# Mixture of experts on one core: the 48-row block of the down product in plain fp32 on two column halves, and a second buffer for the raw down weights

## The chip, the cores and the metric

The kernel runs on one core of a Trainium2 chip. The metric is the device time of one execution in microseconds. Engines: TensorE (PE; its weight loads are PEld), VectorE (DVE), ScalarE (ACT), GpSimd (POOL), and SyncE (SP), whose queue issues most DMAs. Most executions of one kernel agree within 0.3%.

## What is computed

One decoder layer over 1024 positions of width 1024: a mixer of three head groups, cross-attention to 256 memory tokens, and a grouped mixture of experts, each followed by a layer norm. The change touches the last part alone:

```
scores = sigmoid(t @ router_w)               # 16 experts in 4 groups
group  = best group by the sum of its two best biased scores
expert_idx = the two best experts of that group; gate = their scores / their sum
for e in range(16):
    h = silu(t @ w_gate[e]) * (t @ w_up[e])  # 1024 -> 256
    y = y + combine[:, e:e + 1] * (h @ w_down[e])   # 256 -> 1024
x = layer_norm(alpha * x + y)
```

All arrays are fp32.

## The kernel before

The kernel has six phases (`project`, `prepare`, `attend`, `cross_attend`, `experts`, `overflow`), each a block in which every engine runs its own program and waits on semaphores. `cross_attend` ends by scattering each token's row of x (1024 values and its gates) to two slots of a DRAM table, `slot_rows`: one of the 176 slots (`CAP`) of each of its two experts. `experts` then goes over the 16 experts in turn, 176 rows each, as a block of 128 rows and a block of 48 (`ROWS`, `B1`). The 16 turns are written as a `step` per engine; `steps` runs the first four and the last two outright and the other ten in a hardware loop of two steps per turn. The order of the work is the order of each engine's program; there is no planner.

The experts run in the order first of each of the four groups, second of each, and so on, and a token's two experts lie in one group. A step adds the weighted down product to the rows that came with the expert and stores the sum (z) in `slot_sums`. In the first four steps (`NG`, `lowest`) that is all. From the fifth on, POOL first gathers, for each row whose token had its other expert earlier, that expert's stored sum (`gather_low`, L1873), and after the sum the step takes the layer norm, and POOL scatters it to the output for the rows that are now complete (L1900).

TensorE in one step, in order (`step` from L1940):
- gate and up product (L1948) in plain fp32: 32 products of 128 weight columns and 176 moving columns, into the banks `hps`;
- `turn` (L1929, L1931): transposes of the next expert's rows, of which 8 are 128 x 128 and 8 are 48 x 48, after a wait for `rows_loaded`;
- `down` (L1953 to L1962): the product of h (256) with the down weights (two halves of 512 output columns). h and the weights are split into a high part rounded to fp32r and a low part, and hi·hi + hi·lo + lo·hi is summed: 3 products for each of 2 halves of the contraction (`f`), and of the four `UNITS`: (128 rows, columns 0 to 511), (128 rows, 512 to 1023) and the same of the 48 rows. That is 24 products in fp32r of 512 moving columns each. The units use the PSUM banks 0, 1, 2 and 0 of `yps`, so the fourth waits until VectorE has taken the first (`z_made`).

A plain fp32 product appears in the trace as two records each of LDWEIGHTS and MATMUL, an fp32r product as one.

ScalarE takes silu, rounds h (L2002), copies the transposed rows to `xgT`, rounds the next expert's down weights (L1988, `split_down`) and takes squares for the norm (L2015). VectorE multiplies silu by up (L2072), takes the low part of h (L2074), makes the layer norm's output of the expert before (L2041), adds and weighs the four units as they leave PSUM (L2091, `z_made`), centres them (L2052) and takes the low part of the next down weights (L2026).

SP's queue in one step, in order: the raw down weights of the next expert (1 MB) into the only buffer `dn_raw`, after the split of this expert's (L1835); gate and up weights (2 MB) of the expert after next, after this gate and up product (L1838); two stores of z (L1842); the two fetches of the rows of the expert after next (`fetch`, L1824), 128 rows and 48 rows. As the wait for the split of the next weights comes late in the step, the down load of a step follows the row fetches of the step before.

In the retention of `prepare`, TensorE also has products of 64 rows of contraction (L527), whose operands lie in partitions 0 to 63 for two heads and 64 to 127 for the other two; in program order both of the first come ahead of both of the second.

Of the kernel before, what the change touches and what calls it, by code (L numbers as in the profile page):

```python
# [6 lines left out]
f32 = mybir.dt.float32  # L7
# [8 lines left out]
P = 128  # L16
# [15 lines left out]
CAP = 176  # L32
# [1143 lines left out]
def cross_attend(nc, k):  # L1176
# [73 lines left out]
    with nc.psum_tensor("x_tps", [P, 2, 512], f32) as tps, nc.psum_tensor("x_qps", [P, 512], f32) as qps, \  # L1250
# [6 lines left out]
        @block.sync  # L1257
        def _(sp):
            sp.wait_ge(q_lo, KD)
            for s in range(XH):  # L1260
                sp.dma_start(rawo[:, s, :], A["xa_wo"][s * P:(s + 1) * P, :]).then_inc(o_loaded, 16)
            sp.dma_start(rw[:], A["router_w"].rearrange("(s p) e -> p s e", p=P)).then_inc(rw_loaded, 16)
            sp.dma_start(rb[:], over(A["router_bias"], [P, NE])).then_inc(loaded, 16)
            sp.wait_ge(v_sum, 2)
            sp.dma_start(g[:], over(A["ln_xa_g"], [P, D])).then_inc(loaded, 16)
            sp.dma_start(b[:], over(A["ln_xa_b"], [P, D])).then_inc(loaded, 16)

            sp.wait_ge(w_lo, XH)
            sp.dma_start(k.e_dn[:], A["w_dn"][0].rearrange("s p n -> p s n")).then_inc(k.dn_loaded, 16)
# [472 lines left out]
def experts(nc, k):  # L1742
# [10 lines left out]
    g, b_ = k.g3, k.b3  # L1753
    gate_up, dn_raw = k.e_gu, k.e_dn
    xT = k.xgT
    hh = at("h", 143, [P, 2, CAP])
    act_g = at("silu_g", 144.5, [P, 2, CAP])
    hhi = at("h_hi", 146, [P, 2, CAP], f32r)
    hlo = at("h_lo", 147.5, [P, 2, CAP], f32r)
    slot_id = at("slot_number", 149, [P, NE, 2])  # L1760
# [25 lines left out]
    UNITS = [(0, 0), (0, 1), (1, 0), (1, 1)]  # L1786
    BANK = [0, 1, 2, 0]

# [21 lines left out]
    with nc.psum_tensor("rowsT_ps", [P, 3, 512], f32) as tps, nc.psum_tensor("h_ps", [P, 2, 512], f32) as hps, \  # L1810
# [3 lines left out]
        @block.sync  # L1814
        def _(sp):
            k.any_over["sp"] = sp.value_load(k.over_flag[0:1, 0:1], min_val=0, max_val=2 * S)
            def hold(sem, value):

                sp.wait_ge(sem, value)
                sp.sem_inc(held_sp, 1)  # L1820

            def fetch(row, b):
                for c in range(2):
                    sp.dma_start(rows[b][0:ROWS[c], c, :], k.xs_dram[bass.ds(row + c * P, ROWS[c]), :]).then_inc(rows_loaded[b], 16)  # L1824

            sp.wait_ge(k.rows_scattered, 16 * 2 * NT)
            sp.wait_ge(fields_cleared, 2)
            for e in range(2):
                fetch(e * CAP, e)

            def step(n, h, g_, e, b):
                last = is_one_of_last(e, 1)
                if not last:
                    hold(dn_lo_done, n(4, 4))
                    sp.dma_start(dn_raw[:], A["w_dn"][bass.ds(n(1, 1), 1)].rearrange("a s p n -> p (a s) n")).then_inc(dn_loaded, 16)  # L1835
                if not is_one_of_last(e, 2):
                    hold(gsum, n(2, 2))
                    sp.dma_start(gate_up[:, b], A["w_gu"][bass.ds(n(1, 2), 1)].rearrange("a s p n -> p (a s) n")).then_inc(gu_loaded[b], 16)  # L1838
                hold(z_stored, n(32, 128))
                for c in range(2):  # L1840
                    hold(z_made, n(4, 2 * c + 6))
                    sp.dma_start(k.z_dram[bass.ds(n(CAP, c * P), ROWS[c]), :], z[c][:]).then_inc(z_stored, 16)  # L1842
                if not is_one_of_last(e, 2):
                    hold(placed_at, n(1, 1))
                    fetch(n(CAP, 2 * CAP), b)

            steps(sp, step)
# [77 lines left out]
        def _(pe):  # L1925
# [12 lines left out]
            def step(n, h, g_, e, b):  # L1938
# [15 lines left out]

                def down(u, f):
                    c, j = UNITS[u]
                    w = 2 * f + j
                    hi, lo = (t[:, f, c * P:c * P + ROWS[c]] for t in (hhi, hlo))
                    out = yps[0:ROWS[c], BANK[u], :]
                    pe.matmul(out, hi, dn_hi[:, b, w, :], start=(f == 0), stop=False)  # L1960
                    pe.matmul(out, hi, dn_lo[:, b, w, :], start=False, stop=False)  # L1961
                    return pe.matmul(out, lo, dn_hi[:, b, w, :], start=False, stop=(f == 1))  # L1962

                pe.wait_ge(dn_lo_done, n(4, 4))
                pe.wait_ge(hlo_done, n(2, 1))
                for u, free in ((0, 4), (1, 2), (2, 3)):
                    pe.wait_ge(z_made, n(4, free))
                    down(u, 0)
                pe.wait_ge(hlo_done, n(2, 2))
                for u in range(3):  # L1970
                    down(u, 1).then_inc(ysum, 1)
                pe.wait_ge(z_made, n(4, 5))
                down(3, 0)
                down(3, 1).then_inc(ysum, 1)

# [3 lines left out]
        def _(act):  # L1979
# [6 lines left out]
            def split_down(b):  # L1986
                for s in range(4):
                    act.activation(dn_hi[:, b, s, :], dn_raw[:, s, :], ACT.Copy).then_inc(dn_hi_done, 1)  # L1988

            act.sem_inc(ysum, 8)  # L1990
            act.wait_ge(stats_cleared, 6)
            act.wait_ge(dn_loaded, 16)
            split_down(0)
            def step(n, h, g_, e, b):
                last = is_one_of_last(e, 1)
                for m in range(2):
# [4 lines left out]
                    act.wait_ge(ysum, n(4, 8))  # L2001
                    act.activation(hhi[:, m, :], hh[:, m, :], ACT.Copy).then_inc(hhi_done, 1)  # L2002
# [18 lines left out]
        def _(dve):  # L2021
            k.any_over["dve"] = dve.value_load(k.over_flag[0:1, 0:1], min_val=0, max_val=2 * S)
            def split_down(b, n):
                for s in range(4):
                    dve.wait_ge(dn_hi_done, n(4, s + 1))
                    dve.tensor_tensor(dn_lo[:, b, s, :], dn_raw[:, s, :], dn_hi[:, b, s, :].bitcast(f32), ALU.subtract).then_inc(dn_lo_done, 1)  # L2026

# [40 lines left out]
            def step(n, h, g_, e, b):  # L2068
                last = is_one_of_last(e, 1)
                for m in range(2):  # L2070
                    dve.wait_ge(silu, n(2, m + 1))
                    dve.tensor_tensor(hh[:, m, :], act_g[:, m, :], hps[:, m, CAP:2 * CAP], ALU.mult).then_inc(hmul, 1)  # L2072
                    dve.wait_ge(hhi_done, n(2, m + 1))
                    dve.tensor_tensor(hlo[:, m, :], hh[:, m, :], hhi[:, m, :].bitcast(f32), ALU.subtract).then_inc(hlo_done, 1)  # L2074
                    if last:
# [199 lines left out]
def program(nc, A, upto=99):  # L2275
# [47 lines left out]
    k.e_dn = at("e_down_raw", 89, [P, 4, 512])  # L2323
    k.gu_loaded, k.dn_loaded = [k.sem("gate_up_loaded_even"), k.sem("gate_up_loaded_odd")], k.sem("down_loaded")
    k.g3, k.b3 = at("ln3_g", 97, [P, D]), at("ln3_b", 101, [P, D])
# [57 lines left out]
```

## Time and profile before

| | |
|---|---|
| median of 3 runs | 1002.26 us (999.42 to 1003.21) |
| profiled execution, span | 1000.8 us |
| TensorE busy | 967.3 us, 97% |
| weight loads busy | 833.9 us, 83% |
| VectorE busy | 590.3 us, 59% |
| ScalarE busy | 350.6 us, 35% |
| GpSimd busy | 190.4 us, 19% |
| mean granted TensorE clock | 0.992 |
| gate and up product of the experts (L1948) | 155.4 us busy |
| DMA | 151.60 MB, mean 151 GB/s |

The profile is one execution; its own time is its span, from the first to the last instruction. Busy times of one engine overlap those of the others and are shares of that span. The experts' phase runs from about 720 us to the end. In the trace, a matmul record's length includes the way through the array, so records of back-to-back matmuls overlap; the distance from start to start is what one costs. A load's time "to landing" counts from its issue.

### The profile page before, as it was taken

Reading aid. Unit: us, or ns where it says so; the run is one execution under the profiler, and the core shown is the slowest. Engines: PE = TensorE matmul, PEld = TensorE weight load, DVE = VectorE, ACT = ScalarE, POOL = GpSimd, SP = SyncE. Lnnn points to the kernel's source line nnn. Section 1 sums busy time; section 2 is a strip of 40 time slices with the busy share of each in tenths; the row PEclk is TensorE's granted clock in tenths of the full one; section 3 lists DMA queues with packets and bytes.
Section 4 is the critical chain, followed back from the end, with each engine's and each line's share of the span. In section 5 each row is a group of like instructions: output and inputs, shape, how many; then the busy total and the mean of one; then the engine's idle time right before and its main releaser. Section 6 shows DMA issues by size and latency. Waiting matters only on the chain. (4 is left out here: it accounts for less than half of the span.)

```text
span 1000.8 us, 15741 instructions
## 1 busy us (share of the span) xinstructions
PE 967.3 (97%) x5687; PEld 833.9 (83%) x5687; DVE 590.3 (59%) x1271; ACT 350.6 (35%) x737; POOL 190.4 (19%) x248
## 2 busy tenths in 40 slices
PE   7999999999899999999999999999999999999995
PEld 6899888777778999988886888888888989898984
DVE  7744341678466666555557455458634376767676
ACT  6123031435365444430005333331223243434342
POOL 0012100112042110002220000002400134343335
PEclk9999999999899999999999999999999999999998
DMA  9122010001799200160023200032788888989872
GB/s 310 52 85 84 1 64 1 1 1 55 290 412 355 97 22 23 64 253 1 1 84 109 105 1 1 1 129 101 294 276 297 269 311 284 305 306 323 320 277 94
DMA packets 67278, 151.60 MB, mean 151 GB/s; under 512 B 8720, under 2 KB 16144, under 8 KB 67216
## 3 DMA queue, kind: packets, MB, share of 16 engines
q1 hardware_dynamic: 59920, 133.82, 38.0%
q0 software_dynamic: 7296, 16.95, 4.4%
q8 instruction: 39, 0.64, 0.3%
q14 instruction: 23, 0.19, 0.1%
HBM read 107.62 MB, written 52.03 MB: 160 GB/s over the span
## 5 line engine op out<-in xcount | busy, mean ns | idle before, releaser
L1948 PEld LDWEIGHTS h_ps<-xgT,e_gate_up 128*128 128x128 f32 x1024 | 153.9, 190 | 4.5 <-issue 2.2
L1948 PE MATMUL h_ps<-xgT,e_gate_up 128*128 128x176 f32 x1024 | 155.4, 313 | 2.2 <-DVEq L2056 2.2
L262 PE MATMUL unit_ps<-whi,xhi 128*128 128x512 f32 (+1 forms) x256 | 98.3, 384 | 6.2 <-DVE wlo L294 6.2
L263 PE MATMUL unit_ps<-wlo,xhi 128*128 128x512 f32 (+1 forms) x256 | 98.0, 383 | 0.0
L264 PE MATMUL unit_ps<-whi,xlo 128*128 128x512 f32 (+1 forms) x256 | 98.0, 383 | 0.0
L1001 PEld LDWEIGHTS o_ps<-mla_v,prob_T 128*128 128x128 f32 x576 | 70.0, 193 | 9.3 <-issue 6.0
L1001 PE MATMUL o_ps<-mla_v,prob_T 128*128 128x64 f32 x576 | 71.5, 274 | 3.7 <-ACT prob_T L1073 3.5
L262 PEld LDWEIGHTS unit_ps<-whi,xhi 128*128 128x128 f32 x256 | 48.7, 190 | 13.8 <-DVE xlo L338 6.1
L2091 DVE SCALAR_TENSOR_TENSOR z<-y_ps,slot_weight,x_rows 128x512 f32<-128x512 f32 (+1 forms) x64 | 45.7, 746 | 21.7 <-PE y_ps L1962 20.8
L264 PEld LDWEIGHTS unit_ps<-whi,xlo 128*128 128x128 f32 x256 | 48.6, 190 | 7.9
L263 PEld LDWEIGHTS unit_ps<-wlo,xhi 128*128 128x128 f32 x256 | 48.7, 190 | 7.7
L1960 PE MATMUL y_ps<-e_dn_hi,h_hi 128*128 128x512 f32 (+1 forms) x128 | 52.0, 406 | 0.1
L1962 PE MATMUL y_ps<-e_dn_hi,h_lo 128*128 128x512 f32 (+1 forms) x128 | 50.2, 392 | 0.0
L1061 ACT ACTIVATE prob<-s_ps,neg_max 128x640 f32<-128x640 f32 (+3 forms) x32 | 30.5, 954 | 56.2 <-issue 52.6
L1961 PE MATMUL y_ps<-e_dn_lo,h_hi 128*128 128x512 f32 (+1 forms) x128 | 50.1, 391 | 0.0
L1138 DVE COPY prob_T<-t_ps 128x512 f32<-128x512 f32 (+3 forms) x48 | 30.0, 624 | 21.9 <-PE t_ps L988 21.8
L2072 DVE TENSOR_TENSOR h<-silu_g,h_ps 128x176 f32<-128x176 f32 x32 | 10.6, 333 | 53.0 <-ACT silu_g L1999 53.0
L2015 ACT ACTIVATE ln_junk<-z,z_neg_mean 128x1024 f32<-128x1024 f32 (+1 forms) x24 | 27.6, 1150 | 40.8 <-DVE z_neg_mean L2046 37.5
L1999 ACT ACTIVATE silu_g<-h_ps 128x176 f32<-128x176 f32 x32 | 10.2, 318 | 89.3 <-PE h_ps L1948 82.0
L1122 DVE TENSOR_TENSOR s_ps<-s_ps,constants 128x128 f32<-128x128 f32 (+1 forms) x48 | 16.5, 343 | 40.4 <-PE s_ps L979 25.4
L2026 DVE TENSOR_TENSOR e_dn_lo<-e_down_raw,e_dn_hi 128x512 fp32r<-128x512 f32 x64 | 39.8, 678 | 0.8 <-ACT e_dn_hi L1988 0.8
L988 PE MATMUL t_ps<-constants,prob 128*128 128x128 f32 x288 | 40.1, 276 | 0.0
(337 smaller groups left out, 2133.1 us busy)
## 6 DMA issues: line engine op xcount, KB each, us to landing
e_gate_up<-w_gu SPq DMA_DIRECT2D x16, 2048.0 KB, 10.4
e_down_raw<-w_dn SPq DMA_DIRECT2D x16, 1024.0 KB, 5.6
slot_rows<-zeros SPq DMA_DIRECT2D x22, 522.0 KB, 6.2
slot_sums<-zeros SPq DMA_DIRECT2D x22, 512.0 KB, 6.3
x_rows<-slot_rows SPq DMA_DIRECT2D x16, 522.0 KB, 4.7
slot_sums<-z SPq DMA_DIRECT2D x16, 512.0 KB, 4.4
wraw<-w_in SPq DMA_DIRECT2D x24, 256.0 KB, 4.8
xraw<-xT SPq DMA_DIRECT2D x16, 256.0 KB, 4.9
```

Source lines behind the costliest of these rows:

```text
L262: pe.matmul(o, hi, whi[:, s, 0:w], start=(s == 0), stop=False)
L263: pe.matmul(o, hi, wlo[:, s, 0:w], start=False, stop=False)
L264: last = pe.matmul(o, lo, whi[:, s, 0:w], start=False, stop=(s == KD - 1))
L988: last = pe.transpose(tps[:, j, m * P:(m + 1) * P], prob[:, u % 2, j, m * P:(m + 1) * P], ident)
L1001: last = pe.matmul(ops[:, i % 2, h * MV:(h + 1) * MV], probT[:, u % 2, j, (m - a) * P:(m - a + 1) * P], k.v[:, m, h * MV:(h + 1) * MV], st ...
L1061: act.activation(prob[:, u % 2].rearrange("p j n -> p (j n)")[:, 0:(i + 1) * P], sps[:, u % 2].rearrange("p j n -> p (j n)")[:, 0:(i + 1) ...
L1948: end = pe.matmul(hps[:, m, gu * CAP:(gu + 1) * CAP], gate_up[:, b, s, w], xT[:, s, :], start=(s == 0), stop=(s == KD - 1))
L1960: pe.matmul(out, hi, dn_hi[:, b, w, :], start=(f == 0), stop=False)
L1961: pe.matmul(out, hi, dn_lo[:, b, w, :], start=False, stop=False)
L1962: return pe.matmul(out, lo, dn_hi[:, b, w, :], start=False, stop=(f == 1))
L2026: dve.tensor_tensor(dn_lo[:, b, s, :], dn_raw[:, s, :], dn_hi[:, b, s, :].bitcast(f32), ALU.subtract).then_inc(dn_lo_done, 1)
L2091: dve.scalar_tensor_tensor(z[c][:, f], yps[r, BANK[u], :], wgt[r, b, c:c + 1], rows[b][r, c, f], ALU.mult, ALU.add, accum_out=zsum[r, c, j ...
```

## The change

The 48-row block no longer uses the split. Its product is taken in plain fp32 from h itself (`hh`) and from the raw down weights, 4 products in place of 12: the columns 0 to 511 go to partitions 0 to 47 of bank 2, the columns 512 to 1023 to partitions 64 to 111 of the same bank, which are the two halves of the array's columns. The two come in turn for each half of the contraction, and one signal of two comes after the last. As the raw weights are now read by TensorE until the end of the step, they have two buffers. The load for the expert after next is issued at the end of a step, between the stores of z and the fetches of rows; the load for the second expert goes ahead of the loop. The 128-row block is computed as before, with its two units first; the high and low parts of h are kept for its 128 columns only.

```diff
-    hhi = at("h_hi", 146, [P, 2, CAP], f32r)
-    hlo = at("h_lo", 147.5, [P, 2, CAP], f32r)
+    hhi = at("h_hi", 146, [P, 2, P], f32r)
+    hlo = at("h_lo", 147.5, [P, 2, P], f32r)
...
-    BANK = [0, 1, 2, 0]
+    BANK = [0, 1, 2, 2]
+    FROM = [0, 0, 0, 64]
...
+            sp.dma_start(dn_raw[1][:], A["w_dn"][1].rearrange("s p n -> p s n")).then_inc(dn_loaded[1], 16)
             def step(n, h, g_, e, b):
-                last = is_one_of_last(e, 1)
-                if not last:
-                    hold(dn_lo_done, n(4, 4))
-                    sp.dma_start(dn_raw[:], A["w_dn"][bass.ds(n(1, 1), 1)].rearrange("a s p n -> p (a s) n")).then_inc(dn_loaded, 16)
                 if not is_one_of_last(e, 2):
                     hold(gsum, n(2, 2))
                     sp.dma_start(gate_up[:, b], ...).then_inc(gu_loaded[b], 16)
...
                 if not is_one_of_last(e, 2):
+                    hold(ysum, n(4, 12))
+                    sp.dma_start(dn_raw[b][:], A["w_dn"][bass.ds(n(1, 2), 1)].rearrange("a s p n -> p (a s) n")).then_inc(dn_loaded[b], 16)
                     hold(placed_at, n(1, 1))
                     fetch(n(CAP, 2 * CAP), b)
...
-                for u, free in ((0, 4), (1, 2), (2, 3)):
-                    pe.wait_ge(z_made, n(4, free))
-                    down(u, 0)
+                for j in range(2):
+                    pe.wait_ge(z_made, n(4, j + 1))
+                    down(j, 0)
                 pe.wait_ge(hlo_done, n(2, 2))
-                for u in range(3):
-                    down(u, 1).then_inc(ysum, 1)
-                pe.wait_ge(z_made, n(4, 5))
-                down(3, 0)
-                down(3, 1).then_inc(ysum, 1)
+                for j in range(2):
+                    down(j, 1).then_inc(ysum, 1)
+                pe.wait_ge(z_made, n(4, 4))
+
+                for f in range(2):
+                    for u in (2, 3):
+                        j = UNITS[u][1]
+                        end = pe.matmul(yps[FROM[u]:FROM[u] + B1, BANK[u], :], hh[:, f, SMALL], dn_raw[b][:, 2 * f + j, :], start=(f == 0), stop=(f == 1))
+                end.then_inc(ysum, 2)
...
-                    act.wait_ge(dn_loaded, n(16, 32))
+                    act.wait_ge(dn_loaded[1 - b], h(16, 16 * (1 + b)))
...
-                    dve.scalar_tensor_tensor(z[c][:, f], yps[r, BANK[u], :], wgt[r, b, c:c + 1], rows[b][r, c, f], ALU.mult, ALU.add,
+                    dve.scalar_tensor_tensor(z[c][:, f], yps[FROM[u]:FROM[u] + ROWS[c], BANK[u], :], wgt[r, b, c:c + 1], rows[b][r, c, f], ALU.mult, ALU.add,
```

## Rows read from the trace of the kernel before

**Rows 1.** Busy time by period: a light one, a heavy one
```profile
739.12:755.86 16.74, 16.74 (x106) 14.71 (x106) 6.94 (x18) 4.88 (x11) 0.41 (x2) 1.00 0.81 264
856.18:872.93 16.75, 16.75 (x106) 14.72 (x105) 11.93 (x24) 7.37 (x15) 6.52 (x8) 1.00 0.91 305
```
(Columns: the stretch and its length in us; busy time and instructions of PE, PEld, DVE, ACT, POOL; granted clock, DMA share, GB/s.)

**Rows 2.** TensorE's waits, 700 to 980 us: total, times, longest
```profile
PE h_ps L1948 <- DVEq L2056: 2.2, 1, 2.2
PE rowsT_ps L1929 <- DMA x_rows<-slot_rows: 1.9, 1, 1.9
```

**Rows 3.** TensorE in order of time: start, length, line, operation, count
```profile
849.74 0.27 PE L1929 MATMUL rowsT_ps<-constants,x_rows 128*128 128x128 f32 x1
849.95 0.69 PE L1931 MATMUL rowsT_ps<-constants,x_rows 48*128 48x48 f32 x8
850.57 0.49 PE L1960 MATMUL y_ps<-e_dn_hi,h_hi 128*128 128x512 f32 x1
850.90 0.39 PE L1961 MATMUL y_ps<-e_dn_lo,h_hi 128*128 128x512 f32 x1
...
856.18 9.71 PE L1948 MATMUL h_ps<-xgT,e_gate_up 128*128 128x176 f32 x64
865.73 1.04 PE L1929 MATMUL rowsT_ps<-constants,x_rows 128*128 128x128 f32 x8
...
882.47 1.04 PE L1929 MATMUL rowsT_ps<-constants,x_rows 128*128 128x128 f32 x8
```

**Rows 4.** Plain fp32, 512 moving columns, cross-attention phase, in order of time
```profile
525.68 6.17 PE L1407 MATMUL x_acc<-xa_wv_raw,memT 128*128 128x512 f32 x14
```

**Rows 5.** Plain fp32 in the whole array and in row halves, `prepare`
```profile
196.09 1.06 PE L563 MATMUL banks<-lat_T,w_ukv 128*128 128x128 f32 x8
...
189.04 0.72 PE L527 MATMUL banks<-qk_T 64*128 64x128 f32 x8
```

**Rows 6.** Issues of SP's queue in order of time: start, length
```profile
757.20 1.03 SPq L1824 DMA_DIRECT2D x_rows<-slot_rows  x2
759.15 0.38 SPq L1835 DMA_DIRECT2D e_down_raw<-w_dn  x1
...
858.01 0.92 SPq L1824 DMA_DIRECT2D x_rows<-slot_rows  x2
...
866.12 0.38 SPq L1838 DMA_DIRECT2D e_gate_up<-w_gu  x1
...
874.75 0.92 SPq L1824 DMA_DIRECT2D x_rows<-slot_rows  x2
...
891.50 0.94 SPq L1824 DMA_DIRECT2D x_rows<-slot_rows  x2
```

**Rows 7.** Loads issued 755.8 to 772.5 us: count, size, us to landing
```profile
e_down_raw<-w_dn SPq DMA_DIRECT2D x1, 1024.0 KB, 6.5
...
x_rows<-slot_rows SPq DMA_DIRECT2D x1, 195.8 KB, 5.6
```

**Rows 8.** Loads issued 857 to 873 us
```profile
e_gate_up<-w_gu SPq DMA_DIRECT2D x1, 2048.0 KB, 11.0
...
x_rows<-slot_rows SPq DMA_DIRECT2D x1, 195.8 KB, 6.6
```

**Rows 9.** Loads issued 873 to 889.8 us
```profile
x_rows<-slot_rows SPq DMA_DIRECT2D x1, 195.8 KB, 5.2
```

**Rows 10.** Loads issued 890 to 906 us
```profile
x_rows<-slot_rows SPq DMA_DIRECT2D x1, 195.8 KB, 6.9
```

**Rows 11.** VectorE in a heavy period, in order of time
```profile
866.27 0.34 DVE L2072 TENSOR_TENSOR h<-silu_g,h_ps 128x176 f32<-128x176 f32 x1 [2.97 <-ACT silu_g L1999]
...
873.13 0.74 DVE L2091 SCALAR_TENSOR_TENSOR z<-y_ps,slot_weight,x_rows 48x512 f32<-48x512 f32 x1 [0.63 <-PE y_ps L1962]
```

**Rows 12.** VectorE in the last expert, in order of time
```profile
988.21 0.74 DVE L2091 SCALAR_TENSOR_TENSOR z<-y_ps,slot_weight,x_rows 48x512 f32<-48x512 f32 x1
...
988.88 1.27 DVE L2052 SCALAR_TENSOR_TENSOR ln_tmp<-z,z_neg_mean,ln_g 128x1024 f32<-128x1024 f32 x1
```

More of the change, by code:

```diff
@@ L1268, in _ @@
             sp.wait_ge(w_lo, XH)
-            sp.dma_start(k.e_dn[:], A["w_dn"][0].rearrange("s p n -> p s n")).then_inc(k.dn_loaded, 16)
+            sp.dma_start(k.e_dn[:], A["w_dn"][0].rearrange("s p n -> p s n")).then_inc(k.dn_loaded[0], 16)
             sp.dma_start(k.g3[:], over(A["ln_moe_g"], [P, D])).then_inc(k.gains_loaded, 16)
@@ L1753, in experts @@
     g, b_ = k.g3, k.b3
-    gate_up, dn_raw = k.e_gu, k.e_dn
+    gate_up, dn_raw = k.e_gu, [k.e_dn, at("e_down_raw_odd", 150, [P, 4, 512])]
+    SMALL = slice(P, CAP)
     xT = k.xgT
@@ L1953, in step, with down @@
                     turn(1 - b, h(32, 32 * (1 + b)))
-                def down(u, f):
-                    c, j = UNITS[u]
+                def down(j, f):
                     w = 2 * f + j
-                    hi, lo = (t[:, f, c * P:c * P + ROWS[c]] for t in (hhi, hlo))
-                    out = yps[0:ROWS[c], BANK[u], :]
+                    hi, lo, out = hhi[:, f, :], hlo[:, f, :], yps[:, j, :]
                     pe.matmul(out, hi, dn_hi[:, b, w, :], start=(f == 0), stop=False)
@@ L1987, in split_down @@
                 for s in range(4):
-                    act.activation(dn_hi[:, b, s, :], dn_raw[:, s, :], ACT.Copy).then_inc(dn_hi_done, 1)
+                    act.activation(dn_hi[:, b, s, :], dn_raw[b][:, s, :], ACT.Copy).then_inc(dn_hi_done, 1)
             act.sem_inc(ysum, 8)
             act.wait_ge(stats_cleared, 6)
-            act.wait_ge(dn_loaded, 16)
+            act.wait_ge(dn_loaded[0], 16)
             split_down(0)
@@ L2001, in step @@
                     act.wait_ge(ysum, n(4, 8))
-                    act.activation(hhi[:, m, :], hh[:, m, :], ACT.Copy).then_inc(hhi_done, 1)
+                    act.activation(hhi[:, m, :], hh[:, m, 0:P], ACT.Copy).then_inc(hhi_done, 1)
                 if not last:
@@ L2025, in split_down @@
                     dve.wait_ge(dn_hi_done, n(4, s + 1))
-                    dve.tensor_tensor(dn_lo[:, b, s, :], dn_raw[:, s, :], dn_hi[:, b, s, :].bitcast(f32), ALU.subtract).then_inc(dn_lo_done, 1)
+                    dve.tensor_tensor(dn_lo[:, b, s, :], dn_raw[b][:, s, :], dn_hi[:, b, s, :].bitcast(f32), ALU.subtract).then_inc(dn_lo_done, 1)
             def know_high(e, b):
@@ L2073, in step @@
                     dve.wait_ge(hhi_done, n(2, m + 1))
-                    dve.tensor_tensor(hlo[:, m, :], hh[:, m, :], hhi[:, m, :].bitcast(f32), ALU.subtract).then_inc(hlo_done, 1)
+                    dve.tensor_tensor(hlo[:, m, :], hh[:, m, 0:P], hhi[:, m, :].bitcast(f32), ALU.subtract).then_inc(hlo_done, 1)
                     if last:
@@ L2323, in program @@
     k.e_dn = at("e_down_raw", 89, [P, 4, 512])
-    k.gu_loaded, k.dn_loaded = [k.sem("gate_up_loaded_even"), k.sem("gate_up_loaded_odd")], k.sem("down_loaded")
+    k.gu_loaded, k.dn_loaded = [k.sem("gate_up_loaded_even"), k.sem("gate_up_loaded_odd")], [k.sem("down_loaded_even"), k.sem("down_loaded_odd")]
     k.g3, k.b3 = at("ln3_g", 97, [P, D]), at("ln3_b", 101, [P, D])
```

## The prediction

> **What bounds the kernel now.** I read a table of single expert periods first, then who TensorE waits for, then TensorE's order of work, and last the loads, because the change also moves one. An expert takes 16.75 us, and TensorE is busy for all of it at full granted clock, in a light period (experts 0 to 3: no gather, no output) as in a heavy one (experts 4 to 15), while the DMA engines are busy for 0.81 and 0.91 of it [rows 1]. Between 700 and 980 us TensorE waited twice, 2.2 and 1.9 us, at the phase's start [rows 2]. So the phase is the sum of TensorE's instructions: gate and up 9.55 us, transposes of the next rows 1.6, down product 5.5 [rows 3]. What shortens the down product shortens the period, as long as all that TensorE waits for keeps pace. I call the start of the transposes, where gate and up have just ended, E; E is 865.73 and 882.47, and 16.75 before and after these 848.98 and 899.22 [rows 3].
>
> **TensorE's part.** Removed per expert: 12 rounded (fp32r) products of the 48-row block. The 24 products of an expert start at 850.57 and the next work at 856.18; the first is 0.10 late (0.33 to the second instead of 0.23), so one is (856.18 - 850.67) / 24 = 0.229 us and twelve are 2.75 us [rows 3].
>
> Added: 4 plain fp32 products of 512 moving columns. Each is two records; fourteen records took 6.17 us, the last one 0.59 long, so one is (6.17 - 0.59) / 13 = 0.43 us and a product 0.86 [rows 4]. One after the other that is 3.44 us, two at a time 1.72. Column halves stand in no row, but row halves do: eight plain records of 64 rows, four in each half of the array, took 0.72 us, against 1.06 for eight full ones [rows 5]. A full record costs (1.06 - 0.27) / 7 = 0.11; three steps of 0.11, the last record's 0.27 and a start of 0.1 give 0.7, and seven steps would give 1.15. So halves of the array do run at once, and records of one half overtake queued ones of the other (in the code, L527, four of one half stand ahead of four of the other). What row halves do not show is two streams of 128 partitions; but an fp32r column passes in 0.229 / 512 = 0.45 ns where plain fp32 takes 0.84 [rows 3, 4], so two plain streams read hardly more per ns than one fp32r stream. I take 1.73 us, which is nearest to the halves' row; the other end is 3.44.
>
> A change of the array's partition is not free. The last full transpose starts at 849.74 and takes 0.11, the 48-row ones start at 849.95 and run 0.03 late; they are 0.06 apart, the last at 850.42, and the first full product is effective at 850.67 instead of 850.48: 0.13 in, 0.19 out [rows 3]. I take 0.17 in and 0.19 out, with bounds of 0 and 0.3 for each. Per expert: -2.75 + 1.73 + 0.36 = -0.66 us, a period of 16.09. Bounds: -1.02, and with 3.44 and 0.6, +1.3.
>
> **The other edits.** The high and low parts of h shrink from 176 to 128 columns, in four short instructions on engines that sit idle for 3 us ahead of the second multiplication of h [rows 11]: nothing, bounds -0.1 and 0 us a period. TensorE's new wait, for the previous expert's four z, is met some 12 us earlier; behind it stands only the block. The last z starts 0.7 us later after the block's end than now, since both 48-row units come due together at 0.74 each [rows 11]; the 3 us of idle time cover it, and without cover it would cost 0.7 a period. Only in the last expert does it count: the third z, at 988.21 now, waits for the whole block, which I put at 989.05 (985.6 + 6 x 0.229 + 0.17 + 1.73 + 0.17), and the centring of 1.27 and the fourth z stand behind it [rows 12]. That is +0.9 us; the switch out, not paid there, returns 0.2: +0.7. SP's new wait, for the down product, is met before it is reached, as it comes after the last z; behind it stand the down load and the row fetches. The load of the second expert's down weights before the loop is behind the first row fetches and takes nothing.
>
> **The moved load.** SP's queue issues per period: gate and up weights at E + 0.4, two z stores, the two row fetches for the expert after next, and last the down weights [rows 6]. The new order puts the 1 MB of down weights between the z stores and the row fetches, and TensorE waits for the rows at its next E. Where do they land now? In three heavy periods the second fetch is issued at 858.57, 875.28 and 892.08 (the end of the pair less 0.36 us of its own issue) and lands 6.6, 5.2 and 6.9 us later: 865.2, 880.5 and 899.0, against an E of 865.73, 882.47 and 899.22 [rows 3, 6, 8 to 10]. The slack is 0.5, 2.0 and 0.2 us. From the E of the period that issued them this is 16.2, 14.8 and 16.5, mean 15.8. The queue is full in between: the gate and up weights, issued at 866.12, need 11.0 us [rows 6, 8].
>
> What does 1 MB in front of them cost? In a light period the second fetch, issued 0.4 after the pair's start at 757.20, lands 5.6 us later at 763.2, and the down weights, issued at 759.15 and queued behind, land at 759.15 + 6.5 = 765.6: 2.4 us for the megabyte [rows 6, 7]. In heavy periods, where the queue is full since the gate and up load, the new landing is E + 15.8 + 2.4 = E + 18.2. Bounds: E + 17.2, if the closed gap behind the rows gives 1 us back, and E + 19.4, if the low gather's data now meets them. Unstalled, the next E comes 16.09 later: the rows are 2.1 us late. A stall delays the next E and with it the next big load, but not what is queued already, so two periods sum to 16.09 + 18.2 and the mean is 17.15 us. In light periods both loads were down at 765.6, where E was 882.47 - 8 x 16.75 = 748.5, so at E + 17.1, and will be so in the new order; with the emptier first of them I take 16.9 for the four. Nothing else is queued behind TensorE's longer wait than its own down product; the next gate product follows it.
>
> **The sum**, against the profiled execution (span 1000.8 us): first period -0.66; four light ones +0.15 each, +0.6; ten heavy ones (17.15 - 16.75), +4.0; the end +0.7. Together +4.6: 1005.4. The runs' median is 1.5 above that span, so 1006.9 us. The gain on TensorE is there, and the row fetch takes it.
>
> **Rivals.**
> A. The fetch stays hidden. If the rows land by E + 16.09 all the same, the 15 periods give 15 x 0.66 = 9.9, the end takes 0.7 back: 9.2, 993 us. For it: a slack of 2.0 us in one period of three. Against: 0.5 and 0.2 in the other two.
> B. The halves do not overlap (slower). A period has 16.09 + 1.72 = 17.8 us of TensorE work; heavy ones are (17.8 + 18.2) / 2 = 18.0, light ones, whose stores also move, 18.3: 1.1 + 6.2 + 12.5, and 2.6 at the end, +22.4, 1024 us. It decides from 2.4 us for the block on, where TensorE alone is no faster than before. Against it stand the row halves [rows 5]; for it, that no row shows two full-height streams.
> C. Matmuls start strictly in program order (slower). The code issues two records of one half, two of the other, and again; in order they make five slots of 0.43, 2.15 us: 0.43 more in the first period and the end, and with the stalls some 5 us in all, 1012 us. Against it: in order the row halves would need six steps, 6 x 0.11 + 0.37 = 1.03 us, where 0.72 was measured [rows 5].
>
> The Trainium skill, TensorE: Matmul & The Clock Gate, Part 3, "The mechanism", says that matmuls keep program order in start and end and only weight loads are pulled ahead. By that rule C holds and the time is 1012. The trace disagrees, with 0.72 us for the eight.
>
> The Trainium skill, DMA: Bandwidth & Descriptors, "HWDGE ordering", says that each engine consumes a queue's descriptors in ring order. By that the rows wait for the megabyte; were it otherwise, A would hold, 993. The trace agrees: gate and up, issued at 866.12, land at 877.1, the rows, issued at 875.28, at 880.5.
>
> **How the numbers follow.** Chances: forecast 0.68, A 0.15, B 0.10, C 0.07. What can be told from no change is 0.5%, 5 us: 997.3 to 1007.3. The forecast's own range, from the bounds E + 17.2 and E + 19.4, is half of these per heavy period, 5 to 6 us either way: 1001 to 1013; somewhat under half of it lies above 1007.3. Faster: A and a sliver of the forecast, 0.16. Slower: B, C and the forecast's upper part, 0.42. Same: 0.42. For 8 in 10 I leave out B above and most of A below: 996 to 1014.
>
> **What would show it.** Two y records about 0.01 us apart, four such pairs 0.43 apart, and some 2.1 us from the last 128-row product's end to the next gate product. Waits of TensorE's transposes for x_rows in most heavy periods, 1 us in the mean, 8 to 14 us in all, with heavy periods of 17.15 in the mean. The forecast is wrong if these waits stay under 3 us in all (A), or if the block's records follow 0.43 apart without a partner (B) or make five slots (C).

## The result: 2.4% slower, 26 us above the forecast

| | before | changed |
|---|---|---|
| median of the runs | 1002.48 us (4) | 1033.59 us (4; 1022.12 to 1038.4) |
| ratio to before | 1 | 1.0236 [1.0193, 1.028] |
| profiled execution | span 1000.8 | 1034.58, span 1032.8 |
| to the first gate product | 720.05 | 724.30 |
| first gate product to that of the last expert | 253.54 | 278.00 |
| from there to the end | 27.2 | 30.5 |

The forecast was 1006.9 us, 996 to 1014. One of the four changed runs (1038.4), two of e10 and two of e12 below were in a slower state: the ratios are of the other runs alone, whose medians are 1032.6, 1025.3 and 1031.3 us. The medians of this first set give a ratio nearer 1.03 than the recorded 1.0236, and the same kernel gave 1.0172 and 1.02 on two other chips (e8, e12): the loss is 1.7 to 3%. I read the profile after in the order of the one before.

**Periods.** TensorE over the 15 periods between the first gate product and the last expert's; then the stretch from one turn to the next, which ends in a wait, and the stretch after that wait (changed kernel; columns as in [rows 1]):

```profile
724.30:1002.30 278.00, 257.00 (x1501) 213.68 (x1501) 157.79 (x336) 100.22 (x210) 86.68 (x98) 0.94 0.80 271
803.70:823.20 19.50, 16.28 (x101) 13.58 (x100) 14.37 (x28) 7.90 (x17) 5.83 (x6) 1.00 0.83 270
823.20:843.30 20.10, 19.34 (x101) 16.01 (x101) 9.88 (x22) 6.98 (x15) 7.41 (x8) 0.83 0.67 233
```

The kernel before over the same 15 periods:

```profile
720.05:973.59 253.54, 251.69 (x1561) 220.77 (x1562) 157.78 (x338) 101.66 (x210) 68.56 (x94) 1.00 0.86 295
```

TensorE has 60 instructions fewer and is busy 5.3 us longer: the granted clock is 0.94 where it was 1.00, so part of the phase runs at 1.2 GHz, not 2.4. Length less busy time is 21.0 us, where it was 1.85. These are two losses, and the second and third line show how one follows the other: 101 instructions, 16.28 us of work at clock 1.00, in a stretch of 19.50; then, after 3.23 us of waiting, as many instructions take 19.34 us at 0.83.

**Waits of TensorE**, 700 to 1010 us, against [rows 2]:

```profile
PE rowsT_ps L1930 <- DMA x_rows<-slot_rows: 20.9, 13, 3.6
PE h_ps L1949 <- DVEq L2059: 2.2, 1, 2.2
```

**TensorE in order of time**, one block and one late turn, against [rows 3]:

```profile
808.31 1.92 PE L1976 MATMUL y_ps<-e_down_raw,h 128*48 128x512 f32 x8
810.16 9.81 PE L1949 MATMUL h_ps<-xgT,e_gate_up 128*128 128x176 f32 x64
823.21 1.97 PE L1930 MATMUL rowsT_ps<-constants,x_rows 128*128 128x128 f32 x8 [3.23 <-DMA x_rows<-slot_rows]
```

The block of eight records takes 1.92 us, and the next gate product follows its start by 1.85: what was forecast. The eight transposes after the wait take 1.97 us, against 1.04 in [rows 3]: half the clock.

The first and the last turn of the ten heavy periods, each the start of one block of transposes:

```profile
803.71 0.55 PE L1930 MATMUL rowsT_ps<-constants,x_rows 128*128 128x128 f32 x3
991.90 0.69 PE L1930 MATMUL rowsT_ps<-constants,x_rows 128*128 128x128 f32 x2 [3.64 <-DMA x_rows<-slot_rows]
```

(The views end within the block of eight.) That is 188.19 us for ten turns, 18.8 from turn to turn, where the forecast had 17.15.

**SP's queue and the landing**, against [rows 6, 8]. Issues first, then the loads issued 806 to 815 us:

```profile
812.76 0.40 SPq L1844 DMA_DIRECT2D e_down_raw<-w_dn  x1
813.50 1.24 SPq L1826 DMA_DIRECT2D x_rows<-slot_rows  x2
```

```profile
e_down_raw<-w_dn SPq DMA_DIRECT2D x1, 1024.0 KB, 8.3
x_rows<-slot_rows SPq DMA_DIRECT2D x1, 522.0 KB, 7.6
x_rows<-slot_rows SPq DMA_DIRECT2D x1, 195.8 KB, 8.8
```

The second of the two fetches is issued at 814.40 and takes 8.8 us, not 5.2 to 6.9: it lands at 823.2, when the turn starts.

**The end.** SP's wait for TensorE's sequencer at the exit of the last block, before and changed:

```profile
SPq L2158 <- PEq L2158: 0.7, 1, 0.7
```

```profile
SPq L2161 <- PEq L2161: 3.6, 1, 3.6
```

### The profile page after: what moved, and what is told of

Same layout as the page of the kernel before. It is cut to its first block and busy times, and to the rows that moved or that the text cites. A ratio compares the mean times of both kernels' runs of the same rounds, so it can differ in the third digit from the quotient of the medians.

```text
span 1032.8 us, 15607 instructions
## 1 busy us (share of the span) xinstructions
PE 977.2 (95%) x5623; PEld 830.0 (80%) x5623; DVE 591.4 (57%) x1271; ACT 349.1 (34%) x737; POOL 205.6 (20%) x248
## 5 line engine op out<-in xcount | busy, mean ns | idle before, releaser
L1949 PE MATMUL h_ps<-xgT,e_gate_up 128*128 128x176 f32 x1024 | 158.6, 316 | 2.2 <-DVEq L2059 2.2
L1061 ACT ACTIVATE prob<-s_ps,neg_max 128x640 f32<-128x640 f32 (+3 forms) x32 | 30.5, 954 | 56.2 <-issue 52.6
L1138 DVE COPY prob_T<-t_ps 128x512 f32<-128x512 f32 (+3 forms) x48 | 30.0, 624 | 21.6 <-PE t_ps L988 21.5
L1867 POOL COPY slot_weight<-x_rows 128x2 f32 (+1 forms) x16 | 14.9, 933 | 122.2 <-PE rowsT_ps L1932 64.5
L1122 DVE TENSOR_TENSOR s_ps<-s_ps,constants 128x128 f32<-128x128 f32 (+1 forms) x48 | 16.5, 343 | 39.6 <-PE s_ps L979 25.4
L1930 PE MATMUL rowsT_ps<-constants,x_rows 128*128 128x128 f32 x120 | 18.1, 299 | 21.0 <-DMA x_rows<-slot_rows 20.9
L1930 PEld LDWEIGHTS rowsT_ps<-constants,x_rows 128*128 128x128 f32 x120 | 14.3, 151 | 24.9 <-DMA x_rows<-slot_rows 24.8
L988 PEld LDWEIGHTS t_ps<-constants,prob 128*128 128x128 f32 x288 | 34.0, 152 | 0.1
```

Source lines behind the costliest of these rows:

```text
L988: last = pe.transpose(tps[:, j, m * P:(m + 1) * P], prob[:, u % 2, j, m * P:(m + 1) * P], ident)
L1061: act.activation(prob[:, u % 2].rearrange("p j n -> p (j n)")[:, 0:(i + 1) * P], sps[:, u % 2].rearrange("p j n -> p (j n)")[:, 0:(i + 1) ...
L1138: dve.tensor_copy(probT[:, v % 2, 0, 0:(z - a) * P], tps[:, 0, 0:(z - a) * P]).then_inc(pT_copied, 1)
L1930: pe.transpose(tps[:, s // 4, (s % 4) * P:(s % 4 + 1) * P], rows[b][:, 0, s * P:(s + 1) * P], ident)
L1949: end = pe.matmul(hps[:, m, gu * CAP:(gu + 1) * CAP], gate_up[:, b, s, w], xT[:, s, :], start=(s == 0), stop=(s == KD - 1))
```

## The experiments

Fifteen experiments, on four chips, each beside runs of the kernel before on the same chip. Its medians there are 1006 to 1010 us and its runs spread over 1.1% (1003.26 to 1014.84 beside e1, for one), so ratios are what is compared; a time in an expectation counts as its ratio to 1002.48. "Waits" is the length of the 15 periods less TensorE's busy time in them; "half clock" is that busy time less what the same instructions take at full clock (240.99 us, e15's stretch below, at clock 1.00; 251.69 for the long block; plus 15 times the difference of the unstalled period where work was added). One or two us in that column need not be the clock: e1 has 1.2 with a granted clock of 1.00 in all its 15 periods.

| kernel | median, us | ratio to before | waits | half clock |
|---|---|---|---|---|
| changed (first result) | 1033.59 | 1.0236 [1.0193, 1.028] | 21.0 | 16.0 |
| e1 rows first | 1013.54 | 1.0048 [1.0019, 1.0078] | 7.4 | 1.2 |
| e2 load order alone | 1026.14 | 1.0189 [1.0144, 1.0234] | 14.1 | 8.8 |
| e3 half ahead | 1019.83 | 1.0111 [1.0071, 1.015] | 12.9 | 10.1 |
| e4 filler of five | 1024.85 | 1.0169 [1.0121, 1.0216] | 2.8 | 2.3 |
| e5 serial block | 1022.79 | 1.017 [1.0117, 1.0224] | 2.1 | 2.9 |
| e6 other program order | 1012.67 | 1.0061 [1.0029, 1.0094] | 9.6 | 6.4 |
| e7 fields on VectorE | 999.09 | 0.9937 [0.9911, 0.9964] | 3.2 | 2.3 |
| e8 changed again | 1025.16 | 1.0172 [1.0123, 1.0221] | 20.8 | 15.3 |
| e9 before, fields on VectorE | 1004.82 | 0.9998 [0.9971, 1.0024] | 1.3 | 1.5 |
| e10 changed, fields on VectorE | 1027.68 | 1.0182 [1.0123, 1.0241] | 21.5 | 8.8 |
| e11 gate and up in two | 998.69 | 0.9939 [0.9907, 0.997] | 1.5 | 1.7 |
| e12 changed, beside e13, e14 | 1032.05 | 1.02 [1.0152, 1.0248] | 20.7 | 15.3 |
| e13 filler of five | 1024.93 | 1.0164 [1.0126, 1.0202] | 2.2 | 2.3 |
| e14 filler of three | 1030.69 | 1.0181 [1.0131, 1.0231] | 12.1 | 8.4 |
| e15 e11, padded | 998.77 | 0.989 [0.985, 0.9931] | 0.8 | 0.0 |

### e1 and e2: the load order with and without the block

e1, the changed kernel with the fetch first:

```
-                    hold(ysum, n(4, 12))
-                    sp.dma_start(dn_raw[b][:], ...)       # 1 MB
                     hold(placed_at, n(1, 1))
                     fetch(n(CAP, 2 * CAP), b)
+                    hold(ysum, n(4, 12))
+                    sp.dma_start(dn_raw[b][:], ...)
```

> The changed kernel with one thing moved: SP issues the two row fetches ahead of the 1 MB of down weights, not behind them. Theory (load and clock): in the changed kernel the rows landed late, the transposes waited 20.9 us for them, and half-clock stretches followed these stalls. With the fetch ahead of the megabyte the rows land near E + 15.8 again, just inside the unstalled period of 16.13, the clock holds, and 15 periods give back about 0.6 us each: 990 to 999 us, waits for x_rows under 5 us in all, no half-clock stretch between 740 and 980 us. Rival (block): the four plain products, two streams of 128 partitions at once, make the throttle lower the clock whatever the loads do. Then half-clock stretches stay (4 of them in the changed kernel between 740 and 1002 us) and the time is 1015 us or more.

> The kernel before with the changed kernel's loads alone: two buffers of raw down weights, the megabyte ahead of the row fetches, and the 48-row block still in its 12 fp32r products. Load and clock: rows come at E + 18.2 against a period of 16.75, so heavy periods are (16.75 + 18.2) / 2 = 17.5 in the mean, 10 x 0.75 + 4 x 0.2 = +8 us, and the clock adds to it after the longest stalls: 1010 to 1027 us, waits for x_rows of 10 us or more. Block: without the plain products nothing lowers the clock and the load costs at most the 8 us: 1003 to 1010 us, with no half-clock stretch between 740 and 980 us.

The 15 periods of e1 and of e2:

```profile
725.20:974.80 249.60, 242.22 (x1501) 203.98 (x1501) 155.05 (x332) 100.25 (x210) 89.91 (x93) 1.00 0.88 296
```

```profile
722.30:996.90 274.60, 260.47 (x1560) 225.14 (x1561) 157.94 (x338) 101.54 (x210) 84.81 (x98) 0.98 0.81 275
```

e1 is 1.2 to 1.9% below the changed kernel (1.0172 to 1.0236 on three chips), its waits fall from 21.0 to 7.4 us, and the half clock goes; e2, which has no plain fp32 block at all, shows waits of 14.1 us, a half clock of 8.8 and 1.0189. So the order of the loads makes most of the loss, and the block does not lower the clock: the rival falls, and e1's forecast of no half clock holds. But e1 misses its time (990 to 999 us) and its waits (under 5 us): it is no faster than the kernel before, though its light periods are 16.05 us. Six of its heavy periods are 16.5 to 17.8, and its end is 36.2 us, 9 longer than before (4.3 of them a wait for h_lo, 3 the last branch, see e15; the rest is not accounted for). Its fetches explain the first: at the turn that starts at 899.16 they are issued 12.6 us later, at 911.76, where e7, below, issues them 8.9 us after its turn (910.02, 918.94).

```profile
909.60 1.82 SPq L1841 DMA_DIRECT2D slot_sums<-z  x2
911.76 0.91 SPq L1826 DMA_DIRECT2D x_rows<-slot_rows  x2
```

The fetch comes first and is late all the same, since the z ahead of it are late. What makes them late was the next question (e7).

### e3: half the megabyte

```
-                    sp.dma_start(dn_raw[b][:], ...)
+                    sp.dma_start(dn_raw[b][:, 0:2], ...)   # 512 KB ahead of the fetch
...
                     fetch(n(CAP, 2 * CAP), b)
+                    sp.dma_start(dn_raw[b][:, 2:4], ...)   # 512 KB behind it
```

> The changed kernel with the down load cut in two: 512 KB ahead of the row fetches, 512 KB behind them. Load and clock: the rows come 1.2 us later than with nothing ahead, near E + 17.0, so heavy periods are (16.13 + 17.0) / 2 = 16.6 in the mean; stalls of about 1 us, too short to bring the clock down often: 994 to 1008 us, between the two orders. Block: 1015 us or more, like the changed kernel.

Between the two orders, as expected (1.0048, 1.0111, 1.0236 for none, half and all of it), but 0.6% above its upper end (1008 us, 1.0055 of the kernel before): I still priced short stalls as harmless. Waits of at most 2.3 us each came with 10.1 us of half clock (granted clock 0.97 over the 15 periods).

### e8, e12, e13, e4, e14: do the waits bring the clock down?

```
                 else:
+                    for _ in range(5):                     # e14: 3
+                        pe.matmul(tps[:, 2, 0:CAP], ident, xT[:, 0, :], start=True, stop=True)
                     turn(1 - b, h(32, 32 * (1 + b)))
```

> The changed kernel, its late rows included, with five unneeded plain fp32 products (176 columns each, about 0.3 us, 1.5 us in all) of TensorE ahead of each wait for the next rows. It only adds work. If the clock drops because TensorE stands idle at the rows, the filler takes the idle time, the clock stays up and the kernel gets FASTER than the changed one: work per period 17.6, rows at E + 18.2, so 17.9 in the mean in heavy periods and 17.6 in light ones, 1001 - 0.7 + 10 x 1.15 + 4 x 0.9 + 1.5, about 1017 us (1011 to 1024), granted clock 0.99. If the clock has nothing to do with the stalls (the block, or drift from run to run), the filler gives nothing back: the changed kernel's 1034 us or more, with its 0.97.

> The changed kernel itself once more, on another chip and beside the others. Load and clock: 1.018 to 1.030 of the kernel before, waits for x_rows of 12 us or more, and half-clock stretches after some of them inside the expert phase. If the first result came from that chip alone: under 1.012, and no such stretches.

> The changed kernel, run beside e13 and e14 on one chip, as their reference. 1.017 to 1.025 of the kernel before.

> e4 again, on the chip of e12: the changed kernel with 1.5 us of unneeded TensorE work ahead of each wait for the rows. If idle time at the rows brings the clock down, 15 x 1.5 = 22 us of added work cost nothing: within 5 us of e12. If not, the work that does not fall into waits (some 5 to 10 us) comes on top and the half-clock stretches stay: 5 to 10 us over e12.

> The same with three products (0.9 us) in place of five: work per period 17.0, rows near E + 18.2, so short waits of about 1 us remain. If idle time brings the clock down, this is the best of the three, 5 to 12 us under e12, with under 7 us lost to half-clock stretches in the expert phase. If not, it lies at e12's time or up to 5 us above.

The result of the changed kernel repeats on two other chips (1.0172, just under the range of e8; 1.02), with the same waits and half clock. e4, at 1.0169, lies in its range (1011 to 1024 us, 1.009 to 1.021). On e12's chip the filler of five makes 22 us of work in the 15 periods and the kernel is no slower, by the medians 6 to 7 us faster (the intervals overlap). The 15 periods, e12 and then e13:

```profile
722.40:999.40 277.00, 256.29 (x1500) 213.24 (x1500) 157.80 (x336) 100.16 (x210) 86.77 (x97) 0.95 0.81 270
```

```profile
722.50:990.30 267.80, 265.56 (x1650) 228.15 (x1650) 157.63 (x336) 100.18 (x210) 87.07 (x94) 0.99 0.83 280
```

150 more instructions, 9.2 us shorter, granted clock 0.99 for 0.95. Idle time at the rows is what brings the clock down; take the idle time away, with the loads in the same order, and it stays up. e14 missed: its 0.9 us leave waits of 12.1 us, up to 2.6 long, and a half clock of 8.4. Its time, 1 us under e12, is nearer to what the rival forecast; only its two columns speak for the theory. Over all sixteen rows of the table the two columns go together: waits of 12 us and more come with 8 to 16 us of half clock, waits of 3.2 and less with 0 to 3. Of the 6 to 7 us between e12 and e13 some 3 belong to the last branch (e15), which is 3 us shorter in e4, e13 and e14.

### e5 and e6: is it the halves?

e5 puts all four products at the first columns of the array, in two banks; e6 changes the order of issue:

```
-                for f in range(2):
-                    for u in (2, 3):
+                for u in (2, 3):
+                    for f in range(2):
```

> The kernel with the rows fetched first (e1), its four plain fp32 products all on the full width's first columns, in two banks, one after the other. If the halves of the array run at once, serial products cost 1.7 us more of TensorE per expert: the unstalled period of e1, 16.05, becomes 17.7 to 17.8, 5 x 1.7 us in the first periods, less in the heavy ones, which another loop already holds at 17 to 17.8 us: some 10 to 18 us over e1, 1.015 to 1.022 of the kernel before. If the overlap were worth nothing, e1's time, 1.005.

> The kernel with the rows fetched first (e1), with the four records of one column half issued ahead of the four of the other half, where e1 alternates two and two. If a record of one half overtakes the queued ones of the other, the block still takes four slots of 0.43 us and the time is e1's, 1.005 of the kernel before, periods of 16.05. If matmuls start in program order, only the last record of the first half and the first of the second run at once: seven slots, 1.3 us more per expert, light periods of 17.3, and 6 to 12 us over e1.

TensorE's block in e5, e1 and e6, in order of time:

```profile
756.16 3.63 PE L1978 MATMUL y_ps<-e_down_raw_odd,h 128*48 128x512 f32 x8
```

```profile
756.79 1.92 PE L1976 MATMUL y_ps<-e_down_raw_odd,h 128*48 128x512 f32 x8
```

```profile
755.92 1.93 PE L1976 MATMUL y_ps<-e_down_raw_odd,h 128*48 128x512 f32 x8
```

Serial, the block takes 1.71 us more, and 14 of e5's 15 periods are 17.76 to 17.79 against 16.05: the halves run at once and are worth 1.74 us a period. In e6 the eight records still take four slots, though the four of one half stand ahead of the four of the other: they start in four pairs 0.43 us apart, 0.01 between the two of a pair. In program order it would be seven slots, 3.2 us. Both expectations held. The Trainium skill, TensorE: Matmul & The Clock Gate, Part 3, "The mechanism", keeps matmuls in program order; the 1.93 us do not agree with it for plain fp32 on two halves. One more thing stands in the table: e5, on TensorE slower than the kernel before, is as fast as the changed kernel on its second chip (1.017), since it never waits.

### e7, e9, e10: the second loop

What holds e1's heavy periods? GpSimd in one of them, then VectorE over the same time:

```profile
928.62 0.52 POOL L1867 COPY slot_weight<-x_rows 128x2 f32 x1 [3.21 <-DMA out<-ln_out,slot_ids]
929.23 3.56 POOL L1869 TENSOR_SCALAR slot_ids<-slot_where 128x4 int32<-128x4 f32 x1
933.87 1.15 POOL L1874 DMA_INDIRECT x_rows<-slot_sums,slot_ids  x1 [1.08 <-issue]
```

```profile
927.81 2.47 DVE L2055 SCALAR_TENSOR_TENSOR ln_tmp<-z,z_neg_mean,ln_g 128x1024 f32<-128x1024 f32 x2
930.21 2.48 DVE L2029 TENSOR_TENSOR e_dn_lo<-e_down_raw,e_dn_hi 128x512 fp32r<-128x512 f32 x4
932.73 0.34 DVE L2075 TENSOR_TENSOR h<-silu_g,h_ps 128x176 f32<-128x176 f32 x1
```

An operation on 128 x 4 elements, 0.24 us when it is alone, takes 3.56 and ends 0.1 us after VectorE's run of big instructions. This happens in five turns of e1, 3.56 us each time. Behind it stands the gather, and for the gather waits the next z, for z the stores and the fetch. Who VectorE waited for in e1, 860 to 1000 us:

```profile
DVE ln_out L2044 <- POOL z_rstd L1898: 21.3, 8, 4.1
DVE z L2094 <- DMA x_rows<-slot_sums,slot_ids: 10.7, 6, 2.4
```

In the kernel before the same instructions come after that run and cost at most 2.0 us, which TensorE's 16.75 covers. The Trainium skill, SBUF — State Buffer, "SBUF: two separate sides", says that a VectorE operation with two inputs in SBUF and a GpSimd operation that reads SBUF lock each other out of a shared pair of ports, for a whole instruction; the trace agrees that one blocks the other, but here GpSimd waited through five instructions in a row, not one.

e7 moves the two small operations to VectorE and lets GpSimd gather first:

```
+                dve.tensor_copy(wgt[:, b, :], rows[b][:, :, bass.ds(col, 1)]...).then_inc(weight_read, 1)
+                dve.wait_ge(placed_at, n)
+                dve.tensor_scalar(low_ids[:, b], where[:, :, 0:1], float(NOWHERE), None, ALU.add).then_inc(low_made, 1)
...
-                    read_fields(n(1, D + 1), n(1, 2), 1 - b)
                     if not (isinstance(e, int) and lowest(e + 1)):
+                        hold(low_made, n(1, 2))
                         hold(z_stored, n(32, 64))
                         gather_low(1 - b)
+                    read_fields(n(1, D + 1), n(1, 2), 1 - b)
```

> The kernel with the rows fetched first (e1), and the next expert's weight and low slot numbers made by VectorE, right after it has placed the rows, not by GpSimd; GpSimd makes only the slot numbers for the output, after it has issued the gather. Theory (gather loop): in e1 the heavy periods are 17.0 to 17.8 us, not 16.05, because a GpSimd instruction of 4 elements that meets VectorE's ln_tmp and e_dn_lo takes 3.56 us in place of 0.24 and holds the gather that the next z waits for. With it gone the gather is issued some 3 us earlier, all periods are 16.05 to 16.3, and the last expert loses its wait of 4.3 us for h_lo: 12 to 16 us under e1, 0.988 to 0.993 of the kernel before. Rival (DMA): the heavy periods are long since the DMA engines cannot move a period's loads and stores in 16.05 us (in the kernel before, 0.91 x 16.75 = 15.2 us busy), so rows and gathers come late whoever issues them: within 4 us of e1, 1.001 to 1.008.

> The kernel before (its loads and its 12 fp32r products) with the one edit of e7: VectorE makes the next expert's weight and low slot numbers, GpSimd gathers first. If TensorE's 16.75 us hold the period there and GpSimd's held-up instruction (0.5 to 1.2 us, up to 2.0) is covered, it changes nothing: 0.998 to 1.002 of the kernel before, and e7's 0.994 is the block's gain. If the edit is a gain of its own, 0.995 or less, and e7 says nothing of the block.

> The changed kernel, the down load still ahead of the row fetches, with the one edit of e7 on GpSimd and VectorE. If the rows are late through the megabyte alone, the stalls and the half-clock stretches stay: 1.012 to 1.022 of the kernel before, waits for x_rows of 12 us or more. If they are late since the gather delays the z and so the stores and fetches behind them, most of the loss goes: 1.000 to 1.008.

e7 is the first version faster than the kernel before: 0.9937 [0.9911, 0.9964], 1.1% under e1. Ten of its periods are 16.05, four 16.2 to 17.0 (the first, 19.7, is the phase's start), and the wait of 4.3 us for h_lo in e1's last expert is 0.8. The DMA rival falls: the same bytes pass in 16.05 us, at a DMA share of 0.91. The same edit does nothing in the kernel before (e9) and nothing in the changed one (e10): each time another loop was longer. e7 stays just short of my estimate of 0.988 to 0.993; 3 us, 0.003, lie at the end of the kernel (e15).

### e11: a shorter queue ahead of the rows

```
-                    sp.dma_start(gate_up[:, b], ...)          # 2 MB, at E
+                    sp.dma_start(gate_up[:, b, 0:4], ...)     # 1 MB, at E
...
+                    sp.dma_start(gate_up[:, b, 4:8], ...)     # 1 MB, behind the down load
```

> The kernel with rows fetched first and fields on VectorE (e7), with the gate and up load cut in two: the first 1 MB where it was, the second behind the row fetches and the down load. The queue ahead of the rows is a megabyte shorter, 2.4 us by the light periods' price: the rows land near E + 13.4 instead of E + 15.8, the waits of 3.0 us for them go, all periods are 16.05: 2 to 4 us under e7, 0.990 to 0.992 of the kernel before. Rival: the second half comes late for its own gate products, 22 us after E, and TensorE waits for gate and up weights instead: 0.994 or more.

As to the rows it held: 13 of 15 periods are 16.05 us (not the first and the last), and TensorE waits for rows in the first turn alone, 0.7 us. The rival shows once, in a wait of 0.7 us ahead of the last expert's gate product, which starts at 965.51: by the trace's semaphore events the second half of its gate and up weights landed at 965.42. The 1.7 us that the edit takes from e7's waits cannot be told in the time: 0.9939 [0.9907, 0.997], not the forecast 0.990 to 0.992, and its interval holds both answers.

### e15: the last branch

```
             steps(pe, step)
+            for _ in range(64):
+                pe.sem_inc(padding, 1)
```

> e11 with 64 semaphore increments of TensorE behind its last expert, off every path: the change took 8 x 8 instructions from TensorE's program (16 for 24 in each of 8 written-out blocks), and these put its last branch back to where it was. If that place costs the 3 to 3.5 us at the end (SP's wait for TensorE's sequencer, 3.4 to 3.9 us in the kernels with the short block, 0.4 to 0.7 in those with the long one or with the filler), the end is 3 us shorter: 0.988 to 0.991 of the kernel before. If it is something else, as e11: 0.993 to 0.995.

The 15 periods and the end of e15, and then SP's wait at the end of e11 and of e15:

```profile
724.40:966.20 241.80, 240.99 (x1500) 204.14 (x1500) 159.51 (x367) 100.19 (x210) 82.39 (x79) 1.00 0.91 307
966.20:994.40 28.20, 14.73 (x86) 12.08 (x84) 18.89 (x34) 6.22 (x12) 15.53 (x13) 0.85 0.32 108
```

```profile
SPq L2167 <- PEq L2167: 4.2, 1, 4.2
```

```profile
SPq L2170 <- PEq L2170: 0.6, 1, 0.6
```

64 more instructions, and the end is 28.2 us for e11's 31.4. The event trace has the instruction itself: TensorE's compare-and-branch over the overflow phase takes 3.4 to 3.9 us in the ten kernels with the short block and nothing added to TensorE's program, and 0.37 to 0.40 in the kernel before, in e2 and e9 (long block), e4, e13 and e14 (filler) and e15. It is the place of that branch in TensorE's program that decides. A row of the DMA view of that stretch goes with it, 1028.8 to 1032.8 us in the changed kernel:

```profile
q8 instruction: 1, 0.02, 1.5%
```

One block of 16 KB on the queue for instructions, at 1029.94, 1.0 us after the branch began and inside its 3.4 us. Such a load lies inside the long branch of all ten kernels, 1.0 to 1.5 us after its start, and inside none of the seven short ones. That the branch waits for this load is read from the seventeen traces; no experiment forced it. e15 is the best version: 0.989 [0.985, 0.9931], 1.1% faster than the kernel before.

## Why the prediction failed

**TensorE's part: right.** Predicted -0.66 us per expert and an unstalled period of 16.09; measured 16.13 at best in the changed kernel and 16.05 in e1, e7, e11 and e15. Pairs on the two halves, four slots of 0.43, block to gate product as said. Rival B is out by the block's 1.92 us, where the same products on one half take 3.63 (e5), and C by the block's four pairs and by e6.

**The order on SP's queue: right in kind.** Fetches wait behind the megabyte and TensorE waits for the rows. The landing was forecast at E + 18.2; from the turn to the landing of the rows for the next one the ten heavy periods take 16.4 to 22.9 us, 18.8 in the mean, the two longest with half clock in them.

**"So two periods sum to 16.09 + 18.2 and the mean is 17.15 us": this step failed first.** I let a stall happen in one period of two, because it delays the next big load but not what is queued. The trace has 13 waits in 15 turns, and the mean of the ten heavy periods is 18.8. The fetch hangs on the z and these on the turn: its second half is issued 10.3 to 10.7 us after the turn starts in seven of the ten, 11.9 to 13.3 us in the three that ran partly at half clock, and lands 6.2 to 9.6 us later. The soonest of these landings comes 16.4 us after its turn, already later than a period of 16.13, so the next turn is late as well, and a late turn moves the fetch behind it. In the sum the 14 periods had 13.8 us of waits (10 x 1.06 + 4 x 0.81) beside the 1.85 that were there; measured are 21.0, of which 17.9 in the ten heavy turns. That is 5 us of the miss.

**What the working did not have: the clock.** The sum put this term at nothing, without a reason, and it is the largest part of the miss: the stalls were priced at their own length. They bring TensorE, which had next to no idle time before, down to half its clock for a while after it, and that cost 16.0 us, nearly as much again. The stretch 823.20 to 843.30 above shows it, e12 and e13 show that the idle time is the cause. [Rows 1 and 2] held the hint: a clock of 1.00 in a phase without waits.

**The end: +0.7 predicted, +3.3 measured.** In the last expert the last normalisation starts 1023.51 - 1002.30 = 21.2 us after the gate product, 20.9 before: +0.3 of the +0.7. The other 3.0 are the last branch, which no row of mine touched.

The account of the profiled executions, 1032.8 - 1000.8 = 32.0 us, where the forecast had 4.6: TensorE's work -10.7 (240.99 - 251.69), waits +19.2 (21.0 - 1.85), half clock +16.0, the end +3.3, together +27.8; and +4.3 before the first gate product, in phases that the change does not touch. That last part is the run's, not the change's: e8 and e12 reach that point at 718.3 and 722.4 us.

**Rival A (993 us) was also wrong.** Its premise, rows in time behind the megabyte, failed by 20.9 us of waits. With the fetch ahead of the megabyte, as in e1, the rows still are not in time, and the ratio is 1.0048: a shorter TensorE period lets GpSimd's small operations meet VectorE's big ones, and the gather's loop takes over. With that loop cut too, and the rows early, the 15 periods give what rival A put on the block and somewhat more: 253.5 to 241.8 us in e15, 11.7 for its 9.9.

Not settled: how long or how frequent a wait must be to cost clock. e1 had seven, up to 1.6 us, at a granted clock of 1.00 throughout; e3 had ten, up to 2.3 us, and lost 10.1 us.

## What to carry to other kernels

Waits on a TensorE that never waited cost more than their length, since the clock can go down with them: 1.4 to 1.8 times in the eight rows of the table with 9.6 us of waits or more (21.5 + 8.8, 14.1 + 8.8, 21.0 + 16.0 us); in e1 (7.4 us) they cost no clock. And a transfer that hangs on the stalled work itself is late in every period, not in every second one. Shortening the bounding engine by 4% paid here only after the next two loops had been shortened too: list them with their slack (here the row fetch with 0.2 us; and the gather, for which z once waited in the kernel before) before the edit. And load what is needed soonest first: the megabyte that was needed a whole period later stood ahead of the rows that were needed at once.

## What the chip showed that I had not expected

- Adding 22 us of useless TensorE work to a stalling kernel did not slow it (1032.05 and 1024.93 us).
- Plain fp32 products on two column halves overtake each other in the queue: four slots for eight records in either order of issue (1.92 and 1.93 us), against 3.63 on one half.
- A GpSimd instruction on 128 x 4 elements is held through a run of five VectorE instructions, 3.56 us for 0.24.
- One branch of TensorE takes 0.4 or 3.4 to 3.9 us by its place in the program; 64 idle instructions bring it back to 0.4. Inside the long one lies a load of 16 KB on the queue for instructions.
